# A layer's front with scaled bands and alternating pooling, and GpSimd's share of latent attention, on one Trainium2 core

## The chip, the cores and the metric

The kernel runs on one core of a Trainium2 chip. The metric is the time of one execution on the device in microseconds (us). The engines are PE (TensorE), DVE (VectorE), ACT (ScalarE), POOL (GpSimd) and SP (the queue that issues most transfers). SBUF is the on-chip memory that all of them read; PSUM, in eight banks, is where PE writes.

## The reference, cut to what matters

512 positions of width 1024, float32. A first block of two layers is followed by a second block with other mixers, which the change doesn't touch.

```python
def rms_norm(x, g):
    return x * lax.rsqrt(jnp.mean(x * x, -1, keepdims=True) + RMS_EPS) * g
...
def pool_mixer(h, w, scale):            # 4 groups of 256 channels, windows 2, 4, 8, 16
    ...
        mean = (c - lag) / jnp.minimum(n_avail, float(win))[:, None]
        outs.append(mean - hf[:, :, g])
    ...
    y = jnp.einsum('bsgc,gcd->bsgd', p, w).reshape(B, S, D)
    return y * scale
...
def mla(...):                           # 8 heads, q and k of 128 + 64 rotary dimensions
    ...
    q_rope = apply_rope(q[..., QK_NOPE_DIM:], cos[:, :, None], sin[:, :, None])
    ...
    o = causal_attention(q, k, v)
    return o.reshape(B, S, N_HEADS * V_HEAD_DIM) @ w_o

for i in range(2):
    h = rms_norm(x, norm_mix[i])
    x = x + (pool_mixer(h, ...) if i % 2 == 0 else mla(h, ...))
    h = rms_norm(x, norm_ffn[i])
    x = x + swiglu(h, w_gate[i], w_up[i], w_down[i])     # silu(h @ gate) * (h @ up) @ down
```

## The kernel before, in words

Every engine has a program of its own, written out by hand; counting semaphores order them against each other. Nothing is reordered by a scheduler: what stands first in an engine's program runs first.

**Products.** Each float32 operand is split into a high part and a low part (the residue). A product is three matmuls into one PSUM bank: high by high, low by high, high by low (`triple`, L1649, L1650, L1651). `chunk` runs 8 of these triples, 24 matmuls, for one tile of 128 output rows and all 512 positions.

**Weights** come in units of 2048 columns (1 MB). SP loads unit n into `w_raw`, slot n % 2; ACT copies it rounded to `w_hi` (`split_hi`, L614), DVE subtracts to get `w_lo` (`split_lo`, L1049). Slots are free again when the products of unit n - 2 are done. Unit 0 holds the pool weights; gate and up units of the first layer follow in turn.

**The front of layer 0.** x comes in two halves, token by row. ACT squares the four tiles of 128 tokens with their sums (L627) and takes the root; DVE takes its reciprocal (L1072) and scales each tile to `h_tok` (L1075). PE transposes x in 32 pieces (L1673) and ACT copies the eight results to `xT` (L633). The pooling of positions is itself a matmul: each 128x128 piece of `h_tok` is multiplied by a banded matrix `band` (L1685), four matmuls for each of eight channel tiles; ACT and DVE split the result (L638, L1080). The pool weights follow: `mixed`, six matmuls for each of eight tiles; DVE adds the result to `xT` (L1087), ACT and DVE split the sum times its gain to `xg_hi` and `xg_lo` (L642, L1090), ACT squares it (L645), and a matmul with ones (L1693) sums the squares over the partitions into bank 7, one for each tile. Six of those stand before the first gate chunk, two behind it. The chunks of gate and up then run; their results are divided by the root of that sum when DVE reads them, so PE need not wait for it, but bank 7 must be read once the sum is complete.

GpSimd computes the rotary angles in this time (L573 to L593) and has 6 instructions late in the second block (L600).

**The latent attention of layer 1.** Heads go in pairs; each pair has one unit of weights of 1664 columns (`heads`, four units), and seven projections: kn0, kn1, va, vb, qn0, qn1 and u, which is the rotary part of both heads' queries. A loop over 32 steps, one for each head and block of 128 queries, runs on all engines; each is some stages apart from the others. In a step PE computes scores, DVE the row maximum and `neg_max` (L1252), ACT the exponential (L764), DVE the normalising (L1259), PE the transposes of the probabilities (L1840), ACT and DVE their split (L774, L1267), PE the product with the values. `after_step` places the projections of the next pair between the steps, `rotary_head` the rotary residue. For u, DVE multiplies the PSUM result by cosine and sine, four products of 64x512 (L1219, L1220), a matmul with a fixed matrix does the turning in the scores, ACT rounds them (L736) and DVE takes the residue (L1230). DVE also does the residue of the next pair's weights in three pieces, in steps 1 to 3 of each even head. `proj_ready` counts all results DVE has read, and tells PE that a bank is free.

Behind the loop come the last heads' outputs, the unit `mla_o` + 1 to + 4 splits (ACT loads another function table before the first), and the output product `out` for eight tiles m, each over eight heads. Six heads of tiles 0 and 1 are done inside the loop.

## Time and profile before

| | us |
|---|---|
| median of 3 runs | 1404.18 (1402.97 to 1404.34) |
| the profiled execution | 1406.12 |
| its span, first to last instruction | 1404.3 |
| PE busy in it | 1328.1 |
| DVE busy | 788.8 |
| ACT busy | 536.7 |
| POOL busy | 33.0 |
| mean granted clock, 1 being 2.4 GHz | 0.983 |

"Busy" is the time in which an engine has an instruction running. An idle stretch is put down to what ended it, the "releaser". Busy times overlap, so they don't add up to the span. A row of the timeline gives start and length; "xN" means N instructions of one form in a row. Matmuls are pipelined: one of 512 columns is shown as 0.39 us but the next starts 0.23 behind it.

### The profile page before, as it was taken

The numbers are of one execution on the slowest core, as the hardware profiler recorded it, in microseconds if no ns is written. First come the engines' busy times: TensorE is split into PE (matmuls) and PEld (weight loads), VectorE is DVE, ScalarE is ACT, GpSimd is POOL, SyncE is SP. The second block draws the span as 40 slices with busy tenths as digits, with TensorE's granted clock in tenths as the row PEclk, the third lists the DMA queues.
The fourth block names the chain that finished last, engine by engine and source line by source line (L and its number), as shares of the span: only waits on it lengthen the run. The fifth ranks groups of instructions, "written<-read, shape, count | busy, mean of one in ns | idle before, by whom it ended". The sixth has DMA issues, their size and how long they took to land.

```text
span 1404.3 us, 16380 instructions
## 1 busy us (share of the span) xinstructions
PE 1328.1 (95%) x6217; PEld 1099.4 (78%) x6217; DVE 788.8 (56%) x1098; ACT 536.7 (38%) x758; POOL 33.0 (2%) x32
## 2 busy tenths in 40 slices
PE   6999999999999888899999999999999999977997
PEld 5788888888877777788888888888887787766876
DVE  5644445444458676564444444545675578876554
ACT  6522233233334444332322222343233445555334
POOL 6000000000000000000000000000000000020000
PEclk9999999999999899999999999999999999979998
DMA  5122322222331100132222322325441211102321
GB/s 207 62 90 91 118 90 90 84 91 83 101 99 55 49 31 31 60 119 92 90 90 91 118 75 83 101 83 144 130 150 61 60 48 28 61 0 99 116 71 60
DMA packets 120888, 119.43 MB, mean 85 GB/s; under 512 B 13500, under 2 KB 117896, under 8 KB 120584
## 3 DMA queue, kind: packets, MB, share of 16 engines
q1 hardware_dynamic: 120840, 118.77, 26.3%
q8 instruction: 32, 0.52, 0.1%
q14 instruction: 16, 0.13, 0.0%
HBM read 114.57 MB, written 4.19 MB: 85 GB/s over the span
## 4 chain that ended last, share of the span: by engine, by line
PE 83%; DVE 9%; ACT 4%; issue 3%; SPq 0%; DMA 0%; DVEq 0%; ACTq 0%
PE psum L1649 25%; PE psum L1650 25%; PE psum L1651 25%; DVE w_lo L1049 1%; PE psum L1998 1%; ACT w_hi L614 1%; PE psum L1984 1%; PE psum L1970 1%; DVE xg_lo L1225 1%; PE psum L2056 1%; PE psum L1693 1%; DVE du L1326 0%; PE psum L2092 0%; DVE row_top L1250 0%; PE psum L1917 0%
## 5 line engine op out<-in xcount | busy, mean ns | idle before, releaser
L1649 PE MATMUL psum<-xg_hi,w_hi 128*128 128x512 f32 x1072 | 426.1, 397 | 2.1 <-DVE xg_lo L1563 2.1
L1651 PE MATMUL psum<-xg_hi,w_lo 128*128 128x512 f32 x1072 | 417.6, 390 | 0.0
L1650 PE MATMUL psum<-xg_lo,w_hi 128*128 128x512 f32 x1072 | 417.4, 389 | 0.0
L1649 PEld LDWEIGHTS psum<-xg_hi,w_hi 128*128 128x128 f32 x1072 | 201.6, 188 | 44.6 <-DVE xg_lo L1563 3.5
L1651 PEld LDWEIGHTS psum<-xg_hi,w_lo 128*128 128x128 f32 x1072 | 201.2, 188 | 42.5
L1650 PEld LDWEIGHTS psum<-xg_lo,w_hi 128*128 128x128 f32 x1072 | 201.5, 188 | 40.6 <-issue 1.4
L1112 DVE TENSOR_TENSOR w_lo<-w_raw,w_hi 128x2048 fp32r<-128x2048 f32 x42 | 96.3, 2292 | 154.4 <-ACT w_hi L667 154.4
L1136 DVE TENSOR_TENSOR w_lo<-w_raw,w_hi 128x2048 fp32r<-128x2048 f32 x32 | 73.3, 2292 | 115.9 <-ACT w_hi L686 115.9
L1649 PE MATMUL psum<-act_hi,w_hi 128*128 128x512 f32 x352 | 137.2, 390 | 0.0
L1651 PE MATMUL psum<-act_hi,w_lo 128*128 128x512 f32 x352 | 137.0, 389 | 0.0
L1650 PE MATMUL psum<-act_lo,w_hi 128*128 128x512 f32 x352 | 136.9, 389 | 0.0
L667 ACT ACTIVATE w_hi<-w_raw 128x2048 fp32r<-128x2048 f32 x42 | 80.4, 1914 | 141.9 <-PE psum L1651 141.9
L1049 DVE TENSOR_TENSOR w_lo<-w_raw,w_hi 128x2048 fp32r<-128x2048 f32 (+4 forms) x59 | 90.8, 1540 | 29.0 <-ACT w_hi L614 28.9
L686 ACT ACTIVATE w_hi<-w_raw 128x2048 fp32r<-128x2048 f32 x32 | 61.2, 1913 | 117.6 <-PE psum L1651 117.6
L614 ACT ACTIVATE w_hi<-w_raw 128x2048 fp32r<-128x2048 f32 (+1 forms) x39 | 73.2, 1876 | 29.7 <-PE psum L1651 29.6
L1649 PEld LDWEIGHTS psum<-act_hi,w_hi 128*128 128x128 f32 x352 | 66.1, 188 | 14.2 <-DVE w_lo L1136 0.6
L1651 PEld LDWEIGHTS psum<-act_hi,w_lo 128*128 128x128 f32 x352 | 66.1, 188 | 13.8
L1650 PEld LDWEIGHTS psum<-act_lo,w_hi 128*128 128x128 f32 x352 | 66.1, 188 | 13.7
L670 ACT ACTIVATE root<-squares 128x512 f32<-128x512 f32 x44 | 27.8, 632 | 100.4 <-DVE squares L1117 100.4
L672 ACT ACTIVATE act_hi<-squares 128x512 f32 (+1 forms) x44 | 27.8, 631 | 89.0 <-DVE squares L1122 89.0
L1119 DVE TENSOR_TENSOR squares<-psum,rstd 128x512 f32<-128x512 f32 x44 | 30.4, 692 | 50.4 <-PE psum L1651 50.4
L1125 DVE TENSOR_TENSOR act_lo<-squares,act_hi 128x512 f32 (+1 forms) x44 | 30.5, 693 | 39.9 <-ACT act_hi L672 39.9
(366 smaller groups left out, 1751.6 us busy)
## 6 DMA issues: line engine op xcount, KB each, us to landing
w_raw<-in_ffn_w_gate SPq DMA_DIRECT2D x22, 1024.0 KB, 5.0
w_raw<-in_ffn_w_up SPq DMA_DIRECT2D x22, 1024.0 KB, 5.0
w_raw<-in_w_in SPq DMA_DIRECT2D x16, 1024.0 KB, 5.5
w_raw<-in_ffn_w_down SPq DMA_DIRECT2D x16, 768.0 KB, 4.8
w_raw<-in_ffn_w_down SPq DMA_DIRECT2D x16, 640.0 KB, 4.5
w_raw<-in_mla_w_o SPq DMA_DIRECT2D x4, 1024.0 KB, 5.0
w_raw<-in_w_out SPq DMA_DIRECT2D x4, 1024.0 KB, 5.1
w_raw<-in_w_ple_gate SPq DMA_DIRECT2D x4, 1024.0 KB, 5.0
```

The lines of the kernel that those rows point to most:

```text
L614: hi = act.activation(w_hi[:, n % 2, c], raw(n)[:, c], ACT.Copy)
L667: act.activation(w_hi[:, n % 2, :], raw(n), ACT.Copy).then_inc(hi_sem, 1)
L670: act.activation(gate_s, gate_z, ACT.Silu).then_inc(ga, 1)
L686: act.activation(w_hi[:, n % 2, :], raw(n), ACT.Copy).then_inc(hi_sem, 1)
L1049: lo = dve.tensor_tensor(w_lo[:, n % 2, c], raw(n)[:, c], w_hi[:, n % 2, c].bitcast(F32), ALU.subtract)
L1112: dve.tensor_tensor(w_lo[:, n % 2, :], raw(n), w_hi[:, n % 2, :].bitcast(F32), ALU.subtract).then_inc(lo_sem, 1)
L1119: dve.tensor_tensor(up_z, bank[2 + c][:, :], rstd[:, :], ALU.mult).then_inc(gd, 1)
L1125: dve.tensor_tensor(act_lo[:, f, :].rearrange("p a t -> p (a t)"), gate_z, act_hi[:, f, :].bitcast(F32).rearrange("p a t -> p (a t)"), ALU ...
L1136: dve.tensor_tensor(w_lo[:, n % 2, :], raw(n), w_hi[:, n % 2, :].bitcast(F32), ALU.subtract).then_inc(lo_sem, 1)
L1649: pe.matmul(o, wh, xh, start=start, stop=False, skip_group_check=True)
L1650: pe.matmul(o, wh, xl, start=False, stop=False, skip_group_check=True)
L1651: return pe.matmul(o, wl, xh, start=False, stop=stop, skip_group_check=True)
```

## The change

**Front.** x arrives as first half, identity, second half; four of the vectors are issued by SP and six by ACT's queue; the band comes after positions and rotary columns. Squares of tokens: tiles 0 and 2 on ACT, 1 and 3 on DVE. The reciprocal root scales the bands (`band_tok`, four instructions of 576 columns) and the pooling matmul takes x itself. x is transposed for seven tiles into seven banks; `xT` is copied by DVE (tiles 0 to 3) and ACT (4 to 7). The pool weights are split in four parts of 512 columns, placed between the splits of the pooled tiles; on PE, five pooled tiles are followed by mixed and pooled tiles by turns. The eight matmuls with ones become one: ACT writes all eight squares to `mix_squares`, DVE adds them in three instructions of 2048, 1024 and 512 columns, and PE's one matmul follows the second gate chunk. Two casts and a product of gains move behind all this on DVE.

**Attention.** For pairs 1 to 3 ACT copies u from PSUM to `rope_in`, and GpSimd computes the four products, the two rotary residues of a pair, and the weight residues: 1664 columns for pairs 1 to 3, and 2048 for the first unit of `mla_o`. Pair 0 stays with DVE.

**Behind the loop.** The splits of `mla_o` + 1 move into the loop's steps 32 (ACT) and 33 (DVE). PE does seven heads of output tile 2 (21 matmuls) before the last head's part of tiles 0 and 1.

```diff
+        mix_squares = h_tok[:, :, :].rearrange("p i (h t) -> p (i h) t", t=T)
...
+        rope_in = sq_sum2[:, :]
...
+        def proj_released(idx):
+            pr, what = PROJ_ORDER[idx]
+            if what == "u":
+                return (sem("rope_turned"), 4) if pr == 0 else (sem("rope_kept"), pr)
+            return sem("proj_ready"), proj_index(pr, what) + 1
...
+            load_vectors(sp, list(ROWS)[0:SP_VECTORS])
             sp.dma_start(pos_i[:, :], a["positions"][0:1, :].to_broadcast([P, T])).then_inc(sem("pos_loaded"), 16)
             sp.dma_start(rope_col[:, :], a["c_rope"]).then_inc(sem("pos_loaded"), 16)
+            sp.dma_start(band[:, :, :, :], a["c_band"]).then_inc(sem("band_loaded"), 16)
+            load(0)
             sp.dma_start(masks0[:, :], a["c_masks"][:, 0, :]).then_inc(sem("mask_loaded"), 16)
-            load(0)
...
+            def heads_split(n):
+                pool.wait_ge(lo_sem, n)
+                pool.wait_ge(hi_sem, n + 1)
+                c = slice(0, head_thirds(n)[-1])
+                pool.tensor_tensor(w_lo[:, n % 2, c], raw(n)[:, c], w_hi[:, n % 2, c].bitcast(F32), ALU.subtract).then_inc(lo_sem, 1)
+                pool.wait_ge(lo_sem, n + 1)
+            def rotary_products(pr):
+                pool.wait_ge(sem("rope_kept"), pr)
+                pool.wait_ge(sem("rope_lo"), 2 * pr)
+                for e in range(2):
+                    r = slice(64 * e, 64 * e + 64)
+                    for half, table in enumerate((cos_t, sin_t)):
+                        if e or half:
+                            pool.wait_ge(sem("rope_turned"), 4 * pr + 2 * e + half)
+                        pool.tensor_tensor(squares[64 * half:64 * half + 64, e, :], rope_in[r, :], table[r, :], ALU.mult)\
+                            .then_inc(sem("rope_turned"), 1)
+                pool.wait_ge(sem("rope_turned"), 4 * pr + 4)
+            def rotary_residue(h):
+                pool.wait_ge(sem("rope_hi"), h + 1)
+                pool.tensor_tensor(xg_lo[:, QR + h % 2, :], squares[:, h % 2, :], xg_hi[:, QR + h % 2, :].bitcast(F32), ALU.subtract)\
+                    .then_inc(sem("rope_lo"), 1)
+                pool.wait_ge(sem("rope_lo"), h + 1)
+            for h in range(HEADS):
+                for ii in range(NB):
+                    if rotary_head(h, ii) is not None:
+                        rotary_residue(rotary_head(h, ii))
+                    if (h // 2 + 1, "u") in after_step(h, ii):
+                        rotary_products(h // 2 + 1)
+                    if h % 2 == 0 and ii == 0:
+                        heads_split(FIRST["heads"] + 1 + h // 2)
...
+            load_vectors(act, list(ROWS)[SP_VECTORS:])
             act.preload_act_table(ACT.Sqrt)
-            for i in range(NB):
+            for i in (0, 2):
...
+            for m in range(4, KD):
+                act.wait_ge(sem("x_turned"), m + 1)
+                act.activation(xT[:, m, :], bank[m][:, :], ACT.Copy).then_inc(sem("xT_late"), 1)
...
+            def weight_split(g):
+                if g == 0:
+                    act.wait_ge(raw_sem[0], loaded(0))
+                act.activation(pool_part(w_hi, g), pool_part(w_raw, g), ACT.Copy).then_inc(*((hi_sem, 1) if g == 3 else mark(f"pool_w_hi{g}")))
...
-                act.wait_ge(sem("mix_added"), m + 1)
-                act.activation(xg_hi[:, m, :], xT[:, m, :], ACT.Copy, scale=gain("norm_ffn", m)).then_inc(sem("mix_act"), 1)
-                if m >= 2:
-                    act.wait_ge(sem("mix_summed"), m - 1)
-                act.activation(squares[:, m % 2, :], xT[:, m, :], ACT.Square).then_inc(sem("mix_act"), 1)
+                last = act.activation(mix_squares[:, m, :], xT[:, m, :], ACT.Square)
+            last.then_inc(*mark("mix_squared"))
...
+                        if pr:
+                            act.wait_ge(sem("proj_done"), idx + 1)
+                            act.activation(rope_in, proj_result(idx), ACT.Copy).then_inc(sem("rope_kept"), 1)
...
+                    if s == NB * HEADS:
+                        split_hi(FIRST["mla_o"] + 1)
...
-            dve.wait_ge(sem("ident_loaded"), 16)
-            dve.tensor_copy(ident_r[:, :], ident[:, :]).then_inc(sem("masks_ready"), 1)
-            dve.wait_ge(sem("mask_loaded"), 16)
-            dve.tensor_copy(causal[:, :], masks0[:, :]).then_inc(sem("masks_ready"), 1)
+            for i in (1, 3):
+                dve.wait_ge(sem(f"x_loaded{i // 2}"), 16)
+                dve.scalar_tensor_tensor(h_tok[:, i, :], x_tok[:, i, :], 1.0, x_tok[:, i, :], ALU.mult, ALU.mult, accum_out=tok_stat[:, 0, i:i + 1])\
+                   .then_inc(sem("tok_squares"), 1)
+            for m in range(3):
+                dve.wait_ge(sem("x_turned"), m + 1)
+                dve.tensor_copy(xT[:, m, :], bank[m][:, :]).then_inc(sem("xT_early"), 1)
+            dve.wait_ge(*at("tok_root"))
+            dve.reciprocal(tok_stat[:, 2, :], tok_stat[:, 1, :]).then_inc(*mark("tok_rstd"))
+            dve.wait_ge(*at("tok_rstd"))
+            dve.wait_ge(sem("band_loaded"), 16)
+            for i in range(NB):
+                dve.tensor_scalar(band_tok[:, i, :, :], band[:, :, int(i == 0), :], tok_stat[:, 2, i:i + 1], None, ALU.mult).then_inc(sem("band_ready"), 1)
+            dve.wait_ge(sem("x_turned"), 4)
+            dve.tensor_copy(xT[:, 3, :], bank[3][:, :]).then_inc(sem("xT_early"), 1)
...
+            mixed_add(4)
+            split_lo(1)
+            mixed_split(0)
+            for m in range(5, KD):
+                mixed_add(m)
+                mixed_split(m - 4)
+            for m in range(4, KD):
+                mixed_split(m)
...
+                if l == 0:
+                    dve.wait_ge(*at("mix_squared"))
+                    half, pair = mix_squares[:, 0:4, :], mix_squares[:, 0:2, :]
+                    dve.tensor_tensor(half, half, mix_squares[:, 4:8, :], ALU.add).then_inc(*mark("mix_halved"))
+                    dve.wait_ge(*at("mix_halved"))
+                    dve.tensor_tensor(pair, pair, mix_squares[:, 2:4, :], ALU.add).then_inc(*mark("mix_quartered"))
+                    dve.wait_ge(*at("mix_quartered"))
+                    dve.tensor_tensor(mix_squares[:, 0, :], mix_squares[:, 0, :], mix_squares[:, 1, :], ALU.add).then_inc(*mark("mix_summed"))
                 dve.wait_ge(*at(f"{tag}_root"))
...
-                        if rotary_head(h, ii) is not None:
-                            rotary(rotary_head(h, ii))
                         for t in after_step(h, ii):
                             proj(*t)
-                        if h % 2 == 0 and ii >= 1:
-                            split_lo(FIRST["heads"] + 1 + h // 2, ii - 1)
+                    if s == NB * HEADS + 1:
+                        dve.wait_ge(lo_sem, FIRST["mla_o"] + 1)
+                        split_lo(FIRST["mla_o"] + 1)
                     if s >= 6 and (s - 6) % NB == NB - 1:
                         head_out((s - 6) // NB)
                 dve.memset(sq_sum[:, :], 0.0).then_inc(*mark("attn_clear"))
                 dve.wait_ge(*at("attn_clear"))
                 for u in range(1, 5):
-                    split_lo(FIRST["mla_o"] + u)
+                    if u > 1:
...
+            for c in range(4):
+                pooled(c)
+                if c == 1:
+                    pe.wait_ge(*at("cols_ready"))
+                    turn_x(7, range(NB)).then_inc(sem("x_turned"), 1)
+            pooled(4)
+            for m in range(KD):
+                mixed(m)
+                if m < 3:
+                    pooled(m + 5)
...
+                            if first and l == j == 0 and c == 1:
+                                pe.wait_ge(*at("mix_summed"))
+                                pe.wait_ge(sem("ones_set"), 1)
+                                pe.matmul(bank[7][:, :], ones[:, :], mix_squares[:, 0, :], start=True, stop=True).then_inc(*mark("mix_stat"))
...
-                        pe.wait_ge(sem("proj_ready"), idx - 1 if idx > len(FIRST_PROJ) else 4)
+                        pe.wait_ge(*proj_released(idx - 2 if idx > len(FIRST_PROJ) else FIRST_PROJ.index("vb")))
...
+                out(2, 0, 7)
                 for m in range(KD):
-                    out(m, 6 if m < 2 else 0, HEADS)
+                    out(m, 6 if m < 2 else 7 if m == 2 else 0, HEADS)
```

The order of the instructions. VectorE before, behind the eighth pooled tile's split to the root of the squares (L1087 adds, L1090 takes residues):

```order
L1049 TENSOR_TENSOR w_lo<-w_raw,w_hi 128x2048
L1087 SCALAR_TENSOR_TENSOR xT<-psum,cols,xT 128x512 x2
L1090 SCALAR_TENSOR_TENSOR xg_lo<-xT,cols,xg_hi 128x512
...
L1090 SCALAR_TENSOR_TENSOR xg_lo<-xT,cols,xg_hi 128x512 x2
L1049 TENSOR_TENSOR w_lo<-w_raw,w_hi 128x2048
L1099 RECIPROCAL rstd<-root 128x512
```

The same place now, from the residue of weight unit 1 on (L1192 adds, L1198 takes residues):

```order
L1142 TENSOR_TENSOR w_lo<-w_raw,w_hi 128x2048
L1198 SCALAR_TENSOR_TENSOR xg_lo<-xT,cols,xg_hi 128x512
L1192 SCALAR_TENSOR_TENSOR xT<-psum,cols,xT 128x512
...
L1198 SCALAR_TENSOR_TENSOR xg_lo<-xT,cols,xg_hi 128x512 x5
L1226 CAST causal<-masks 128x128
L1228 CAST ident_r<-ident 128x128
L1230 TENSOR_TENSOR gain<-cols 128x8
L1142 TENSOR_TENSOR w_lo<-w_raw,w_hi 128x2048
L1240 TENSOR_TENSOR h_tok<-h_tok 128x2048
L1242 TENSOR_TENSOR h_tok<-h_tok 128x1024
L1244 TENSOR_TENSOR h_tok<-h_tok 128x512
L1246 RECIPROCAL rstd<-root 128x512
```

The weight residue and the three adds of the tree now stand between the last residue and the reciprocal, and unit 1's residue stands ahead of most of this, where before it stood ahead of all adds.

In the attention, VectorE before, around the rotary products of the next pair (`row_top`, `neg_max` and `probs` are the step's softmax):

```order
L1267 TENSOR_TENSOR pt_lo<-psum,pt_hi 128x3x128
L1219 TENSOR_TENSOR squares<-psum,cos_t 64x512
L1220 TENSOR_TENSOR squares<-psum,sin_t 64x512
L1219 TENSOR_TENSOR squares<-psum,cos_t 64x512
L1220 TENSOR_TENSOR squares<-psum,sin_t 64x512
L1225 TENSOR_TENSOR xg_lo<-psum,xg_hi 128x2x2x128
L1272 TENSOR_TENSOR o_lo<-psum,o_hi 128x512
L1250 TENSOR_REDUCE row_top<-psum 128x1
```

VectorE now at the same step:

```order
L1409 TENSOR_TENSOR pt_lo<-psum,pt_hi 128x3x128
L1366 TENSOR_TENSOR xg_lo<-psum,xg_hi 128x2x2x128
L1414 TENSOR_TENSOR o_lo<-psum,o_hi 128x512
L1392 TENSOR_REDUCE row_top<-psum 128x1
L1394 TENSOR_TENSOR neg_max<-row_top,rq 128x1
```

GpSimd's program in the attention for the first two units (it had nothing there before):

```order
L627 TENSOR_TENSOR w_lo<-w_raw,w_hi 128x1664
L639 TENSOR_TENSOR squares<-sq_sum,cos_t 64x512
L639 TENSOR_TENSOR squares<-sq_sum,sin_t 64x512
L639 TENSOR_TENSOR squares<-sq_sum,cos_t 64x512
L639 TENSOR_TENSOR squares<-sq_sum,sin_t 64x512
L646 TENSOR_TENSOR xg_lo<-squares,xg_hi 128x512
L627 TENSOR_TENSOR w_lo<-w_raw,w_hi 128x1664
L646 TENSOR_TENSOR xg_lo<-squares,xg_hi 128x512
```

The four products left VectorE's queue for GpSimd's, whose odd head's residue (the second L646) stands behind the next unit's weights.

## Rows read from the trace of the kernel before

**Rows 1.** The page's first part: engine, busy us (share of the span) x instructions.

```profile
PE 1328.1 (95%) x6217; PEld 1099.4 (78%) x6217; DVE 788.8 (56%) x1098; ACT 536.7 (38%) x758; POOL 33.0 (2%) x32
```

**Rows 2.** Windows, front and attention loop: window, length, busy per engine, PEclk, DMA.

```profile
0.00:60.67 60.67, 47.38 (x229) 38.16 (x230) 36.80 (x41) 37.25 (x51) 24.45 (x26) 1.00 0.40 138
449.00:557.00 108.00, 87.60 (x486) 75.82 (x487) 79.22 (x206) 53.34 (x125) 0.00 (x0) 0.94 0.12 38
```

**Rows 3.** Waits, 0 to 16 us: engine line <- releaser: total us, times, longest.

```profile
PE psum L1666 <- DMA vec_rows<-in_conv_b: 10.1, 1, 10.1
```

**Rows 4.** Waits, 446 to 580 us, the attention loop and what follows.

```profile
PE psum L1840 <- DVE pt_lo L1267: 10.3, 10, 2.2
...
PE psum L1649 <- DVE xg_lo L1225: 4.8, 6, 1.1
...
PE psum L1649 <- issue: 3.2, 2, 1.8
```

**Rows 5.** Timeline of the front: start us, us, engine line op out<-in xcount [idle before <-releaser].

```profile
13.38 2.79 DVE L1075 TENSOR_SCALAR h_tok<-x_tok,tok_stat 128x1024 f32<-128x1024 f32 x3
...
15.66 1.09 ACT L633 ACTIVATE xT<-psum 128x512 f32<-128x512 f32 x2
...
39.64 1.02 PE L1693 MATMUL psum<-squares,ones 128*128 128x512 f32 x2
...
40.10 0.80 PE L1649 MATMUL psum<-pooled_hi,w_hi 128*128 128x512 f32 x1
...
43.22 0.80 PE L1649 MATMUL psum<-xg_hi,w_hi 128*128 128x512 f32 x1
...
44.63 1.90 ACT L614 ACTIVATE w_hi<-w_raw 128x2048 fp32r<-128x2048 f32 x1
...
46.56 2.29 DVE L1049 TENSOR_TENSOR w_lo<-w_raw,w_hi 128x2048 fp32r<-128x2048 f32 x1 [1.57 <-ACT w_hi L614]
...
56.26 0.39 PE L1649 MATMUL psum<-xg_hi,w_hi 128*128 128x512 f32 x1
...
61.70 0.39 PE L1649 MATMUL psum<-xg_hi,w_hi 128*128 128x512 f32 x1
```

**Rows 6.** Groups of VectorE, 446 to 580 us: shapes, xcount | busy, mean ns | idle.

```profile
L1049 DVE TENSOR_TENSOR w_lo<-w_raw,w_hi 128x512 fp32r<-128x512 f32 (+3 forms) x13 | 11.4, 879 | 2.9 <-ACT w_hi L614 2.9
...
L1252 DVE TENSOR_TENSOR neg_max<-row_top,rq 128x1 f32<-128x1 f32 x32 | 5.1, 159 | 1.1
...
L1219 DVE TENSOR_TENSOR squares<-psum,cos_t 64x512 f32<-64x512 f32 x6 | 4.1, 686 | 1.1 <-issue 1.0
```

**Rows 7.** Timeline, GpSimd's instructions and VectorE's beside them.

```profile
34.40 1.29 POOL L591 TENSOR_TENSOR angle<-angle 128x512 f32<-128x512 f32 x1
...
34.84 1.39 DVE L1090 SCALAR_TENSOR_TENSOR xg_lo<-xT,cols,xg_hi 128x512 fp32r<-128x512 f32 x1
...
1247.43 8.96 POOL L600 TENSOR_TENSOR pn_lo<-du,pn_hi 64x512 fp32r<-64x512 f32 x6 [1210.72 <-ACT pn_hi L867]
...
1250.11 1.11 DVE L1532 TENSOR_SCALAR du<-du,row_inv 128x1024 f32<-128x1024 f32 x1
```

**Rows 8.** Timeline, weights and first projection of pair 1, u to scores of pair 3.

```profile
450.46 0.82 DVE L1049 TENSOR_TENSOR w_lo<-w_raw,w_hi 128x640 fp32r<-128x640 f32 x1 [0.79 <-ACT w_hi L614]
...
454.45 0.50 PE L1649 MATMUL psum<-ckv_hi,w_hi 128*128 128x512 f32 x1 [1.23 <-DVE w_lo L1049]
...
521.17 0.39 PE L1651 MATMUL psum<-cq_hi,w_lo 128*128 128x512 f32 x1
...
524.97 0.47 PE L1649 MATMUL psum<-cq_hi,w_hi 128*128 128x512 f32 x1 [1.79 <-issue]
...
529.47 0.50 PE L1649 MATMUL psum<-xg_hi 128*128 128x512 f32 x1 [1.01 <-DVE xg_lo L1225]
```

**Rows 9.** Timeline of TensorE behind the loop.

```profile
573.58 0.50 PE L1649 MATMUL psum<-o_hi,w_hi 128*128 128x512 f32 x1 [0.67 <-DVE o_lo L1272]
...
578.48 0.50 PE L1649 MATMUL psum<-o_hi,w_hi 128*128 128x512 f32 x1 [2.53 <-DVE w_lo L1049]
```

More of the change, by code:

```diff
@@ new lines, in mixed_split @@
+            def mixed_split(m):
+                act.wait_ge(sem("mix_added"), m + 1)
+                act.activation(xg_hi[:, m, :], xT[:, m, :], ACT.Copy, scale=gain("norm_ffn", m)).then_inc(sem("mix_hi"), 1)
+            act.wait_ge(*at("cols_ready"))
+            weight_split(0)
+            pooled_split(0)
+            pooled_split(1)
+            weight_split(1)
+            pooled_split(2)
+            pooled_split(3)
+            weight_split(2)
+            pooled_split(4)
+            weight_split(3)
@@ L1068, in _, with weight_split, pooled_split @@
             dve.wait_ge(*at("cols_ready"))
+            def weight_split(g):
+                dve.wait_ge(*((hi_sem, 1) if g == 3 else at(f"pool_w_hi{g}")))
+                dve.tensor_tensor(pool_part(w_lo, g), pool_part(w_raw, g), pool_part(w_hi, g).bitcast(F32), ALU.subtract)\
+                   .then_inc(*((lo_sem, 1) if g == 3 else mark(f"pool_w_lo{g}")))
+            def pooled_split(c):
+                dve.wait_ge(sem("pooled_hi"), c + 1)
+                dve.scalar_tensor_tensor(pooled_lo[:, c, :], bank[POOLED_BANKS[c]][:, :], gain("norm_mix", c), pooled_hi[:, c, :].bitcast(F32),
+                                         ALU.mult, ALU.subtract).then_inc(sem("pooled_lo"), 1)
@@ new lines, in mixed_add, with mixed_split @@
+            def mixed_add(m):
+                if m == 0:
+                    dve.wait_ge(sem("xT_early"), 4)
+                if m == 4:
+                    dve.wait_ge(sem("xT_late"), 4)
+                dve.wait_ge(sem("mixed_done"), m + 1)
+                dve.scalar_tensor_tensor(xT[:, m, :], bank[4 + m % 3][:, :], gain("pool_scale", m), xT[:, m, :], ALU.mult, ALU.add)\
+                   .then_inc(sem("mix_added"), 1)
+            def mixed_split(m):
+                dve.wait_ge(sem("mix_hi"), m + 1)
+                dve.scalar_tensor_tensor(xg_lo[:, m, :], xT[:, m, :], gain("norm_ffn", m), xg_hi[:, m, :].bitcast(F32),
+                                         ALU.mult, ALU.subtract).then_inc(sem("mix_lo"), 1)
@@ L1661, in chunk, with turn_x @@
                 return mm
+            def turn_x(m, blocks):
+                for i in blocks:
+                    mm = pe.transpose(bank[m][:, i * P:(i + 1) * P], x_tok[:, i, m * P:(m + 1) * P], ident[:, :])
+                return mm
             pe.wait_ge(sem("ident_loaded"), 16)
+            pe.wait_ge(sem("x_loaded0"), 16)
+            for m in range(7):
+                turn_x(m, (0, 1))
+            pe.wait_ge(sem("x_loaded1"), 16)
+            for m in range(7):
+                turn_x(m, (2, 3)).then_inc(sem("x_turned"), 1)
@@ L1684, in _ @@
                     n = min(BAND, T - i * P)
-                    mm = pe.matmul(bank[4 + c % 4][:, i * P:i * P + n], h_tok[:, i, c * P:(c + 1) * P], band[:, c // 2, int(i == 0), 0:n],
+                    mm = pe.matmul(bank[POOLED_BANKS[c]][:, i * P:i * P + n], x_tok[:, i, c * P:(c + 1) * P], band_tok[:, i, c // 2, 0:n],
                                    start=i == 0, stop=i == NB - 1, skip_group_check=True)
                 mm.then_inc(sem("pooled_done"), 1)
-            def mix_squares(m):
-                if m == 0:
-                    pe.wait_ge(sem("ones_set"), 1)
-                pe.wait_ge(sem("mix_act"), 2 * m + 2)
-                pe.matmul(bank[7][:, :], ones[:, :], squares[:, m % 2, :], start=m == 0, stop=m == KD - 1, skip_group_check=True).then_inc(sem("mix_summed"), 1)
@@ L1696, in _, with mixed @@
[L1696 to L1699 removed]
+            def mixed(m):
                 g, c = divmod(m, 2)
[L1701 to L1702 removed]
+                wh, wl = hi_tiles(0, 8)
+                pe.wait_ge(*((lo_sem, 1) if g == 3 else at(f"pool_w_lo{g}")))
+                pe.wait_ge(*((sem("xT_late"), m + 1) if m < 3 else (sem("mix_added"), m - 2)))
```

168 lines of the change are left out of this document (75 added, 93 removed).

## The prediction

> **What bounds the kernel now.** I read the page first: TensorE is busy 95% of the span [rows 1]. It is the bound nearly everywhere, so only places where TensorE stands idle, or does work that can be left out, can give time. I then asked for windows over the two stretches that the change touches. In the first 60.67 us TensorE is busy 47.38 us: 13.3 us are open. In the 108 us of the attention loop it is busy 87.60: 20.4 us are open, with VectorE at 79.22, ScalarE at 53.34 and GpSimd at nothing [rows 2]. The waits say what is behind it. At the start TensorE stands 10.1 us for the vectors [rows 3]; in the loop and just behind it 10.3 us for residues of transposed probabilities, 4.8 for residues of projections, 3.2 for "issue", which stands where a projection waits for the bank that VectorE's rotary products read [rows 4]. So the loop is held by VectorE's queue in small pieces, not by its busy share.
>
> The profiled execution took 1406.12 us (span 1404.3). The sum below is made against that span; the median of the runs, 1404.18, lies 1.9 lower, so a span change goes onto the median unchanged. What a measurement here can tell from no change is 0.2%, 2.8 us.
>
> **Part 1, the front.** Before: h_tok (0.93 us a tile, from 13.38) feeds pooling. Mixed products begin only behind the eighth tile, and of the eight ones matmuls six stand among and behind them, two behind the first gate chunk. A ones matmul costs 0.86: 0.46 to the next start (39.64 to 40.10), and the first product behind it 0.4 more than the 0.23 of the others. The first gate chunk starts at 43.22. A chunk is 24 matmuls, 5.44 us (56.26 to 61.70), and the fourth (the second of the up unit) starts at 61.70 [rows 5].
>
> After, walked with these durations (0.7 to 0.75 for a residue or add of 512 columns, 0.66 from start to start):
> - The transposes no longer stand behind the vectors, and hide beside the statistics. Squares end about 9.6 (two engines instead of one), root 9.9, three copies on VectorE, reciprocal 11.8. Four bands of 576 columns, taken at 0.69 from h_tok's 0.93 for 1024, end at 14.6. Pooling starts at 14.9 instead of 15.8.
> - Pooled tile 4, pool weight parts (0.69 each) and residues (0.70) lead to mixed(0) at 20.7. TensorE then owes three pooled tiles and five mixed products, six matmuls or 1.36 us each, and waits for VectorE between: mixed(4) ends near 29.5, its add at 30.1.
> - VectorE next does the residue of weight unit 1, 2.29 us, then six alternating adds and residues at 0.66: 36.5. The first gate chunk can run from 34.7 instead of 43.22.
> - **The new tail of the front**: ScalarE's last xg_hi at 37.2, eight squares at 0.53 (back to back, from 1.09 for two copies) to 41.5, w_hi of unit 2 1.90 to 43.4; VectorE's w_lo 2.29 to 45.7; then the three adds of the tree, 2048, 1024 and 512 wide, 2.29 + 1.2 + 0.69 and their gaps, to 50.0. TensorE has both gate chunks behind it at 46.5 and waits 3.5 us for this sum. The one ones matmul (0.86) is over at 50.9 and the third chunk (5.44) at 56.3; the fourth starts there, against 61.70. **Gain 5.4 us.** Seven ones matmuls less are in it. All else of the front (DMA order, casts moved behind, gain product) lies beside this: the cast of ident is needed in attention first.
>
> Bounds: 6.7 if the tree runs without gaps and squares a little faster; 3.4 if the band, now behind more issues on SP, or the weights come 2 us late.
>
> **Part 2, GpSimd in the attention.** VectorE loses 11.4 us of weight residues (2.29 of them only moved within the tail), twice 4.1 of rotary products (one of the two lines stands in the rows) and six rotary residues of the same 0.69: about 21 us of its 79 [rows 6]. GpSimd gets 12 products of 64x512 at 1.4 (between 1.29, a product of 128x512 alone, and 1.49, a sixth of the 8.96 that six took), six residues at 1.29, three weight residues of 1664 columns at 4.2 (1.29 x 1664/512) and one of 2048 at 5.2: 42.3 us in all [rows 7], none of which was there. What then ends TensorE's waits:
> - *Rotary chain, once in each of three pairs.* Before, the last matmul of u starts at 521.17 and the scores that need the residue start at 529.47 [rows 8]: 7.9 us behind its end, in which TensorE waits 1.79 and 1.01. After: ScalarE copy 0.6, four products 5.6, residue 1.3, hops 0.3: 7.8 us. A wait of much the same length remains. It is at another place, and the odd head's residue, behind GpSimd's next residue of weights, adds 0.7 each time. Waits for rotary and bank: 8.0 before, 12.4 after.
> - *First pair's weights.* VectorE began the residue at 450.46 and did it in three pieces with softmax between; TensorE waited 1.23 for it, until 454.45 [rows 8]. GpSimd in one piece of 4.2 ends at 454.7: +0.3.
> - *Probabilities.* VectorE, at 54% instead of 73%, answers sooner. Of 11 us of waits for pt_lo I take 3.9 as gone, those with a moved instruction ahead in its queue.
> - Sum so far +0.6 to +0.8.
> - *VectorE beside GpSimd.* A VectorE residue from two SBUF inputs, begun at 34.84, took 1.39 instead of the usual 0.74 while GpSimd's product ran from 34.40 to 35.69 [rows 7]: as if it had stood until that was over. In the loop neg_max is such an operation, 32 times on the path from scores to exponential [rows 6]. GpSimd busy 42.3 of 108 us meets 13 of them; the rest of the instruction that they meet is 1.3 us on average (a random point falls oftener into the long weight residues): 17 us held. Each step lasts 3.4 us and VectorE works 1.8 in it, so most is absorbed. Ends: 0 and 17; I take 2.4, a seventh, since the one wait of this kind in the trace cost TensorE nothing that can be seen.
>
> **Loop: +3.0 us**, with ends -6 (all waits for pt_lo and projections go) and +14.
>
> The Trainium skill, "SBUF — State Buffer", section "SBUF: two separate sides", says that VectorE and GpSimd share a port under an exclusive lock, held for the whole instruction when VectorE needs both. The rows above agree. By it, VectorE's normalising of probabilities would be held too, and the sum for the loop would be +10.
>
> **Part 3, behind the loop.** TensorE waited 0.67 at 573.58 and 2.53 at 578.48 for w_lo of mla_o's second unit [rows 9]. The change makes it inside the loop and puts 21 matmuls ahead of the last heads' outputs. Both waits (3.2) go; the third unit's residue, behind the same ScalarE table load, is late next, by 1.0 to 1.5 as TensorE comes sooner. **Gain 2.2** (1.7 to 3.2).
>
> **Sum**: -5.4 + 3.0 - 2.2 = -4.6. Span 1399.7, median 1399.6. The granted clock was 0.94 in the loop [rows 2]; a spell at 1.2 GHz more or less moves this by 1 to 2 us.
>
> **Rivals.**
> 1. *The loop gains as well* (0.15). VectorE's load falls by a quarter and the waits for pt_lo and xg_lo go, 15 us with the bank waits; rotary waits on GpSimd return 8 and holding 3: -4 instead of +3. For it: each of these waits is behind VectorE's queue. Against: the rotary chain is no shorter. -5.4 - 4 - 2.2: 1392.6.
> 2. *The front gives little* (0.21), that is, the change doesn't do what it says there. The sum of squares has moved from eight hidden pieces to one chain of 12.8 us that TensorE waits for; with GpSimd's angle chain beside it, a late band, or half clock behind a 3.5 us pause, it ends 3 us later: -2.2 + 3.0 - 2.2, 1402.8.
> 3. *GpSimd holds VectorE* (0.14), the other side. In the loop neg_max and the normalising wait out whole GpSimd instructions, up to 5.2 us. The price is +10 to +12 in place of +3.0; it decides from +7.6 on, where front and tail are used up; at +11 the sum is +3.4: 1407.6. For it: the row of 1.39. Against: VectorE's scaling with one SBUF input, at 1250.11 amid six GpSimd products, took 1.11 [rows 7], less than one of those.
>
> **How the numbers follow.** Forecast 0.50, covering 1397 to 1402.5. Predicted 1399.6. The range takes in rival 1 down to 1392 and rival 3's nearer half to 1407. Faster by over 2.8 us (under 1401.4): most of the forecast (0.44) and rival 1 (0.15), 0.59. Within 2.8: the forecast's upper edge, nearly all of rival 2 and the mild end of rival 3, 0.28. Slower: the rest, 0.13.
>
> **What the profile of the changed kernel would show.** Right: first gate chunk near 34.7, a TensorE wait of about 3.5 us for the ones matmul, the fourth chunk near 56.3; GpSimd near 75 us busy; waits on GpSimd's rotary residue of 2 to 3.5 us three times; pt_lo waits of 6 to 9 us; no wait of 2.5 behind the loop. Wrong: GpSimd's products far over 1.5 us, neg_max over 1 us many times, a wait over 6 us before the ones matmul, or loop waits well off 23.

## The result, and the profile after

The changed kernel takes 1412.35 us (median of 5 runs, 1411.12 to 1413.80), the kernel before 1402.97 (5 runs, 1400.30 to 1404.34): ratio 1.0069, 95% interval 1.0058 to 1.0080. It is **slower by 9.4 us**; 4.6 less was forecast. The profiled executions differ by less, spans 1410.5 and 1404.3, and the traces below are compared by those: the one of the kernel before took 1406.12 us, 3.2 above its median, so a few us of every comparison with its trace may be that execution's own.

The page's first part, after (against [rows 1]): GpSimd has gained 35 us of work, and VectorE is no less busy.

```profile
PE 1332.8 (94%) x6203; PEld 1105.6 (78%) x6203; DVE 791.8 (56%) x1082; ACT 533.0 (38%) x756; POOL 68.4 (5%) x54
```

**The front, timeline after** (against [rows 5]):

```profile
13.01 2.85 DVE L1167 TENSOR_SCALAR band_tok<-band,tok_stat 128x576 f32<-128x576 f32 x4 [1.30 <-DMA band<-in_c_band]
13.68 4.91 PE L1831 MATMUL psum<-band_tok,x_tok 128*128 128x144 f32 x16 [2.29 <-DVE band_tok L1167]
...
36.55 0.42 PE L1791 MATMUL psum<-xg_hi,w_hi 128*128 128x512 f32 x1
...
40.32 4.26 ACT L734 ACTIVATE h_tok<-xT 128x512 f32<-128x512 f32 x8
...
48.63 2.28 DVE L1240 TENSOR_TENSOR h_tok<-h_tok 128x2048 f32<-128x2048 f32 x1
...
52.96 1.13 PE L1885 MATMUL psum<-h_tok,ones 128*128 128x512 f32 x2 [3.42 <-DVE h_tok L1244]
...
59.40 0.39 PE L1791 MATMUL psum<-xg_hi,w_hi 128*128 128x512 f32 x1
```

The steps stand in the forecast order, and TensorE waits 3.42 us for the sum (forecast 3.5), but all of it is later: VectorE waits 1.30 us behind the reciprocal for the band, and the granted clock from 13 to 21 us is 0.57. The first gate chunk starts at 36.55 (forecast 34.7), the fourth chunk at 59.40 (forecast 56.3, before 61.70). The front gives 2.3 us of the 5.4.

**The loop**, from the first row maximum to the last, the same 492 matmul records in each run. The windows of the kernel before and of the change, columns as in [rows 2]:

```profile
447.16:555.51 108.35, 88.24 (x492) 76.50 (x490) 79.33 (x204) 53.69 (x125) 0.00 (x0) 0.94 0.12 38
```

```profile
444.84:562.54 117.70, 93.82 (x492) 81.75 (x490) 76.69 (x174) 55.20 (x128) 39.15 (x22) 0.87 0.11 35
```

It is 9.35 us longer. TensorE's open time (the time in which no matmul runs) grows by 3.8 (20.1 to 23.9), its busy time for the same matmuls by 5.6, at a granted clock of 0.87 instead of 0.94: about 31 us of this loop ran at 1.2 GHz, and about 13 before. The same window of e1 below, which has the new front and tail but none of GpSimd's work, is shorter than both:

```profile
445.73:547.63 101.90, 82.53 (x492) 71.71 (x490) 79.18 (x204) 53.51 (x125) 0.00 (x0) 1.00 0.14 40
```

Against it the change opens 4.5 us more and its matmuls take 11.3 longer. VectorE has 30 instructions less and hardly less busy time. The groups of VectorE from 445 to 563 us say where it went (mean ns stands behind the busy time):

```profile
L1401 DVE TENSOR_SCALAR probs<-probs,row_inv 128x512 f32<-128x512 f32 (+3 forms) x30 | 21.7, 722 | 1.1
...
L1394 DVE TENSOR_TENSOR neg_max<-row_top,rq 128x1 f32<-128x1 f32 x32 | 12.6, 394 | 1.1
```

neg_max took 5.1 us in all before [rows 6] and takes 12.6. The normalising before, in the group of 446 to 580 us:

```profile
L1259 DVE TENSOR_SCALAR probs<-probs,row_inv 128x512 f32<-128x512 f32 (+3 forms) x32 | 12.4, 387 | 1.1
```

It takes 722 ns each now, 335 more. That is 7.5 and 10 us, against 21 taken away. Nine of the 32 neg_max took over 0.25 us, the longest 1.73. Timeline of one place, VectorE and GpSimd:

```profile
474.92 3.95 POOL L627 TENSOR_TENSOR w_lo<-w_raw,w_hi 128x1664 fp32r<-128x1664 f32 x1 [9.55 <-ACT w_hi L678]
475.16 0.55 DVE L1409 TENSOR_TENSOR pt_lo<-psum,pt_hi 128x384 fp32r<-128x384 f32 x1
...
477.37 0.41 DVE L1392 TENSOR_REDUCE row_top<-psum 128x1 f32<-128x256 f32 x1
477.82 1.07 DVE L1394 TENSOR_TENSOR neg_max<-row_top,rq 128x1 f32<-128x1 f32 x1
478.81 0.15 DVE L1399 RECIPROCAL row_inv<-row_sum 128x1 f32<-128x1 f32 x1
...
478.95 1.26 POOL L646 TENSOR_TENSOR xg_lo<-squares,xg_hi 128x512 fp32r<-128x512 f32 x1
479.00 1.44 DVE L1401 TENSOR_SCALAR probs<-probs,row_inv 128x384 f32<-128x384 f32 x1
```

neg_max, one column wide and 0.16 us long when alone, ends 0.02 us behind GpSimd's instruction; the normalising (0.4 to 0.5 alone) ends 0.23 behind GpSimd's next one. The residue and the maximum that read PSUM run through at their usual 0.55 and 0.41. Waits of TensorE, 440 to 590 us, after (against [rows 4]; pt_lo is the residue of the transposed probabilities, xg_lo that of a projection):

```profile
PE psum L1986 <- DVE pt_lo L1409: 15.9, 13, 2.8
...
PE psum L1791 <- issue: 5.8, 3, 2.8
...
PE psum L1986 <- DVE probs L1401: 1.7, 1, 1.7
```

The waits for pt_lo grew from 10.3 to 15.9; "issue" is now the wait for GpSimd's rotary residue. Those for xg_lo are gone. The last row is new: the first weight residue held a normalising for 3.20 us, and TensorE waited 1.7 for it.

### The profile page after: what moved, and what is told of

It is laid out like the page before. It is cut to its first block, busy times and chain, and to the rows that moved or that the text cites. A ratio compares the mean times of both kernels' runs of the same rounds, so it can differ in the third digit from the quotient of the medians.

```text
span 1410.5 us, 16349 instructions
## 1 busy us (share of the span) xinstructions
PE 1332.8 (94%) x6203; PEld 1105.6 (78%) x6203; DVE 791.8 (56%) x1082; ACT 533.0 (38%) x756; POOL 68.4 (5%) x54
## 4 chain that ended last, share of the span: by engine, by line
PE 82%; DVE 10%; ACT 4%; issue 3%; DMA 1%; SPq 0%; POOL 0%; DVEq 0%; ACTq 0%
PE psum L1791 25%; PE psum L1792 25%; PE psum L1793 25%; DVE w_lo L1142 1%; PE psum L2145 1%; ACT w_hi L678 1%; PE psum L2131 1%; PE psum L2117 1%; DVE probs L1401 1%; PE psum L1831 1%; PE psum L1986 1%; DMA band<-in_c_band 1%; PE psum L2203 1%; DVE du L1468 0%; PE psum L2239 0%
## 5 line engine op out<-in xcount | busy, mean ns | idle before, releaser
L1142 DVE TENSOR_TENSOR w_lo<-w_raw,w_hi 128x2048 fp32r<-128x2048 f32 (+3 forms) x46 | 79.2, 1722 | 26.1 <-ACT w_hi L678 26.1
L1791 PEld LDWEIGHTS psum<-act_hi,w_hi 128*128 128x128 f32 x352 | 66.1, 188 | 14.4 <-DVE w_lo L1283 0.6
L1792 PEld LDWEIGHTS psum<-act_lo,w_hi 128*128 128x128 f32 x352 | 66.1, 188 | 13.6
```

Of the source, the lines that this page charges most:

```text
L1142: lo = dve.tensor_tensor(w_lo[:, n % 2, c], raw(n)[:, c], w_hi[:, n % 2, c].bitcast(F32), ALU.subtract)
L1791: pe.matmul(o, wh, xh, start=start, stop=False, skip_group_check=True)
L1792: pe.matmul(o, wh, xl, start=False, stop=False, skip_group_check=True)
```

## The experiments

Each group of experiments was timed beside its own runs of the kernel before, whose medians were 1402.28 (e1 to e4), 1402.69 (e5 to e8), 1403.43 (e9 to e12) and 1404.14 (e13 to e16). The table gives ratios to those, and for the loop, between the same two instructions as above, its length, TensorE's busy time in it and the granted clock. Medians come from all runs of a kernel, the last three columns from one traced execution each.

| run | front | rotary | weight residues | median us | ratio (95%) | loop | PE busy | clock |
|---|---|---|---|---|---|---|---|---|
| before | old | VectorE | VectorE | 1402.97 | | 108.4 | 88.2 | 0.94 |
| change | new | GpSimd | GpSimd | 1412.35 | 1.0069 (1.0058-1.0080) | 117.7 | 93.8 | 0.87 |
| e2, old tail | new | VectorE | VectorE | 1397.65 | 0.9969 (0.9954-0.9984) | 104.4 | 85.4 | 0.97 |
| e1 | new | VectorE | VectorE | 1397.93 | 0.9967 (0.9954-0.9979) | 101.9 | 82.5 | 1.00 |
| e3 | new | GpSimd | VectorE | 1397.46 | 0.9965 (0.9951-0.9978) | 103.6 | 85.5 | 0.96 |
| e4 | new | VectorE | GpSimd, whole | 1408.67 | 1.0041 (1.0027-1.0054) | 114.3 | 89.5 | 0.93 |
| e5 | new | VectorE | GpSimd, 128 | 1395.85 | 0.9946 (0.9933-0.9958) | 102.1 | 83.3 | 0.98 |
| e11 | new | VectorE | as e5, first VectorE | 1393.78 | 0.9931 (0.9915-0.9946) | 99.3 | 82.1 | 1.00 |
| e16 | new | VectorE | as e11, 256 | 1393.81 | 0.9930 (0.9917-0.9944) | 99.6 | 82.0 | 1.00 |
| e9 | new | GpSimd | GpSimd, 128 | 1414.56 | 1.0076 (1.0062-1.0091) | 120.3 | 93.6 | 0.87 |
| e10 | new | GpSimd | as e9, first VectorE | 1409.61 | 1.0051 (1.0036-1.0066) | 114.0 | 89.1 | 0.93 |
| e13 | new | GpSimd, ahead | GpSimd, 128 | 1399.57 | 0.9977 (0.9968-0.9986) | 106.6 | 86.3 | 0.95 |
| e15 | new | GpSimd, ahead | as e13, first VectorE | 1398.18 | 0.9957 (0.9943-0.9971) | 103.5 | 84.9 | 0.97 |
| e14 | new | GpSimd, ahead | GpSimd, whole | 1418.28 | 1.0103 (1.0088-1.0118) | 124.2 | 95.1 | 0.86 |
| e12, neg_max on ScalarE | new | GpSimd | GpSimd, whole | 1403.09 | 0.9997 (0.9986-1.0008) | 106.9 | 85.6 | 0.95 |

**Parts alone.** e1 undoes GpSimd's share:

```diff
-                    if rotary_head(h, ii) is not None:
-                        rotary_residue(rotary_head(h, ii))
-                    if (h // 2 + 1, "u") in after_step(h, ii):
-                        rotary_products(h // 2 + 1)
-                    if h % 2 == 0 and ii == 0:
-                        heads_split(FIRST["heads"] + 1 + h // 2)
...
+                        if rotary_head(h, ii) is not None:
+                            rotary(rotary_head(h, ii))
...
+                        if h % 2 == 0 and ii >= 1:
+                            split_lo(FIRST["heads"] + 1 + h // 2, ii - 1)
```

> The change without GpSimd's share of the attention: VectorE does the rotary products, their residues and the weight residues in three pieces, as before; the front and the part behind the loop stay changed. Theory H (GpSimd's instructions hold VectorE's neg_max and normalising): the loop is as before, the front gives 2.3 and the tail 2.1 as in the trace of the change, so 4 to 5 us below before, and no neg_max over 0.2 us. Theory R (the rotary chain itself became longer): the same here. Theory C (the clock fell in the loop for another reason, such as the earlier start): the loop stays some 5 us longer, and the time is at or above before.

e2 also restores the part behind the loop; e3 and e4 take back only one half of GpSimd's share.

> The front alone. From the two traces: 2.3 us gained at the second turn of gate and up, so 2 to 3 us below before. If the front had given what was forecast it would be 5.4. The spell at half clock at 13.6 us should be there again if the front's own order makes it.

> As e1, but GpSimd does the rotary products and residues (18 instructions of 1.28 us); weight residues on VectorE. H: it meets neg_max and normalising some 8 times with 0.6 us each and costs 3 to 6 us over e1; the longest neg_max is below 1.4 us. R: all of the 11 us that the loop lost is here.

> As e1, but GpSimd does the weight residues (three of 3.9 us, one of 4.6); rotary on VectorE. H: few but long holds, a normalising of 3 us and neg_max of over 1.5 us; costs 3 to 6 us over e1. R: VectorE is relieved and nothing else changes, so it is at or below e1.

Without GpSimd the change gains 4.4 us, as H said; C falls. Its loop is not "as before", though: 6.5 us shorter in the traces with the same instructions, at a granted clock of 1.00. The front alone (e2) gives 4.6, more than the 2 to 3 expected, and the same as e1, so the part behind the loop gives nothing that these runs can tell. Rotary on GpSimd costs nothing, against both theories, although it held neg_max six times for over 0.25 us, up to 1.21. The weight residues, four instructions of 16.2 us in all, cost 10.7 us, well over H's 3 to 6, and R falls. In e4 each of them held one VectorE instruction: the first a normalising (3.20 us), the others a rotary residue that takes 0.69 alone (3.13, 3.14, 3.81). None of them was a neg_max, against what H said: all 32 took 5.1 us, as before. What stood behind the held instruction in VectorE's queue came late all the same; TensorE's waits for pt_lo in the loop are 13.6 us, in e1 7.8:

```profile
473.70 3.94 POOL L627 TENSOR_TENSOR w_lo<-w_raw,w_hi 128x1664 fp32r<-128x1664 f32 x1 [20.76 <-ACT w_hi L674]
...
475.06 3.13 DVE L1368 TENSOR_TENSOR xg_lo<-squares,xg_hi 128x512 fp32r<-128x512 f32 x1 [0.56 <-ACT xg_hi L819]
```

**Length of GpSimd's instruction.** e5 does the same residues in pieces:

```diff
-                pool.tensor_tensor(w_lo[:, n % 2, c], raw(n)[:, c], w_hi[:, n % 2, c].bitcast(F32), ALU.subtract).then_inc(lo_sem, 1)
+                for c0 in range(0, c.stop, 128):
+                    c1 = slice(c0, min(c0 + 128, c.stop))
+                    part = pool.tensor_tensor(w_lo[:, n % 2, c1], raw(n)[:, c1], w_hi[:, n % 2, c1].bitcast(F32), ALU.subtract)
+                part.then_inc(lo_sem, 1)
```

> As e4 (weight residues on GpSimd, rotary on VectorE), but each residue in pieces of 128 columns, one instruction each. Theory H (VectorE is held until the running GpSimd instruction ends, and gets its turn between two): the longest normalising falls from 3.2 to under 0.9 us and the time to within 3 us of e1. Theory B (both engines share what the memory gives, whatever the length): the time stays at e4's, some 10 us above e1. If GpSimd wins every turn, normalising stays at 3 us and the time too.

12.8 us less than e4, and 2 less than e1. The columns, the data and the place are the same; GpSimd even works longer (25.4 us instead of 16.2 in the loop). So what costs is the length of a hold, not shared bandwidth. Timeline of e5:

```profile
472.28 6.24 POOL L629 TENSOR_TENSOR w_lo<-w_raw,w_hi 128x128 fp32r<-128x128 f32 x13 [19.18 <-ACT w_hi L677]
...
473.63 0.69 DVE L1371 TENSOR_TENSOR xg_lo<-squares,xg_hi 128x512 fp32r<-128x512 f32 x1 [0.56 <-ACT xg_hi L822]
...
475.29 0.21 DVE L1393 TENSOR_TENSOR neg_max<-row_top,rq 128x1 f32<-128x1 f32 x1
...
475.61 0.51 DVE L1400 TENSOR_SCALAR probs<-probs,row_inv 128x384 f32<-128x384 f32 x1
```

VectorE gets its turn between two pieces. One new wait stood in e5, 3.1 us for the first unit's residue:

```profile
PE psum L1792 <- POOL w_lo L629: 3.1, 1, 3.1
```

e11 gives that one unit back to VectorE, e16 takes pieces of 256.

> As e5 (rotary on VectorE, weight residues in pieces on GpSimd), but VectorE does the first weight residue: the wait of 3.1 us goes and VectorE's queue takes 2.2 us more. 0 to 2 us below e5's 1395.9, so about 1394.5.

> As e11, the best so far, with pieces of 256 columns instead of 128: a hold lasts up to 0.7 us instead of 0.4, and GpSimd is done some 1.3 us earlier. Within 1.5 us of e11's 1393.8.

Both as expected (e11 2.1 us below e5, e16 level with it), and the best of all: 0.69% and 0.70% under the kernel before.

**The full change, mended.** e9 is the change with the pieces alone, e10 with the first unit on VectorE too.

> The changed kernel with one edit: GpSimd's weight residues in pieces of 128 columns. Rotary stays on GpSimd, in whole instructions of 1.28 us. Theory H: the long holds are what made it slow, so it falls from 1412 to between 1396 and 1401. If the two parts of GpSimd's work harm each other in another way (a rotary residue queued behind the weight residue), it stays above 1405: in pieces the weight residue takes 5.7 to 7.3 us instead of 3.7 to 4.6, so that queue is longer.

> As e9, but VectorE does the first of the four weight residues, in its three pieces. In e5 TensorE waited 3.1 us for that one alone. 1 to 3 us below e9.

e9 gained nothing, and its waits show why:

```profile
PE psum L1794 <- issue: 13.9, 6, 3.6
PE psum L1989 <- DVE pt_lo L1412: 8.8, 11, 2.1
PE psum L1794 <- POOL w_lo L629: 3.0, 1, 3.0
```

The pieces did their part: the waits for pt_lo fell from 15.9 us to 8.8. But there are six waits for rotary residues instead of the three of 5.8 us in the change, and one for the first unit's residue. e10 is 5.0 us below e9 (1 to 3 expected). Timeline of GpSimd and of TensorE at one of the new ones:

```profile
476.31 5.76 POOL L629 TENSOR_TENSOR w_lo<-w_raw,w_hi 128x128 fp32r<-128x128 f32 x13 [8.57 <-ACT w_hi L681]
482.14 1.26 POOL L649 TENSOR_TENSOR xg_lo<-squares,xg_hi 128x512 fp32r<-128x512 f32 x1
```

```profile
483.51 0.47 PE L1794 MATMUL psum<-xg_hi 128*128 128x512 f32 x1 [2.31 <-issue]
```

The odd head's residue is queued behind the weight residue, and that now takes 5.76 us instead of 3.95. e13 and e14 let it go first, with pieces and without:

```diff
-                    if h % 2 == 0 and ii == 0:
+                    if h % 2 == 0 and ii == 1:
                         heads_split(FIRST["heads"] + 1 + h // 2)
```

> As e9 (full change, weight residues in pieces of 128), but GpSimd does the odd head's rotary residue ahead of the weight residue. Theory Q (the queue on GpSimd is what e9 and e10 pay): the three waits for the odd heads' residues go and the time falls by 8 us or more, to 1400 to 1406. If the holds by the rotary instructions pay for it, it stays above 1410.

> The changed kernel with that one move, weight residues whole. If both theories hold, the queue's part goes and the holds' part stays: 1405 to 1409. Theory H alone: no change from 1412. Theory Q alone: the same as e13.

> As e13, with the first weight residue on VectorE: 2 to 5 us below e13 (e9 to e10 gave 5).

e13 is 15 us below e9: Q holds there, and the two mended together make the full change faster than before (0.9977). The waits for the odd heads' residues are gone:

```profile
PE psum L1794 <- issue: 5.7, 3, 2.8
```

e15 is 1.4 below e13, less than the 2 to 5 expected. With the residues in pieces rotary on GpSimd is no longer free, as it was in e3: e13 and e15 stand about 4 us above e5 and e11, which have it on VectorE (ratios 0.9977 and 0.9957 against 0.9946 and 0.9931). No run says why.

e14 is 6 above the change, against every theory's number: for whole residues the queue cost nothing, and the move brought the long instruction over neg_max itself:

```profile
478.12 3.71 POOL L627 TENSOR_TENSOR w_lo<-w_raw,w_hi 128x1664 fp32r<-128x1664 f32 x1
```

```profile
478.18 3.67 DVE L1394 TENSOR_TENSOR neg_max<-row_top,rq 128x1 f32<-128x1 f32 x1
```

A product of one column takes 3.67 us; the next transposes on TensorE wait 3.46 for what follows from it. The change differs from e14 only in the place of the weight residue in GpSimd's program, and so in what it holds.

**Which VectorE instruction.** e12 gives neg_max to ScalarE:

```diff
-                    dve.wait_ge(sem("att_top"), s + 1)
-                    dve.tensor_tensor(neg_max[:, c], row_top[:, c], rq[:, 1, 2 * i:2 * i + 1], ALU.mult).then_inc(sem("att_max"), 1)
...
+                    act.wait_ge(sem("att_top"), s + 1)
+                    act.activation(neg_max[:, c], row_top[:, c], ACT.Copy, scale=rq[:, 1, 2 * i:2 * i + 1]).then_inc(sem("att_max"), 1)
```

> The changed kernel with one edit: ScalarE computes neg_max, so VectorE has no operation from two SBUF inputs in a step; the normalising stays where it is. If neg_max's holds (some 7 us of 18 in the trace of the change) carry the cost, it falls by 4 us or more; if the holds of the normalising do, it stays within 2 us of 1412.

9.3 us less. The normalising is still held, if less (18.6 us for 30; 21.7 in the change, 11.8 before), so getting neg_max out of VectorE's queue is worth most of the loss. That does not make neg_max's own holds the dear ones: e4 has none and loses 10.7, e3 has six of up to 1.21 us and loses nothing. What is dear comes with GpSimd's instructions of 3.7 to 4.6 us: in e4 and e14 holds of 3.1 us and more, in the change one such hold and then three of 1.1 to 1.7 on neg_max, each followed at once by 1.4 for the normalising under the rotary residue queued behind. The edit also takes VectorE's own work on neg_max away, about 5 us; the two are not told apart here.

**The front's waits.**

```diff
             pe.wait_ge(sem("x_loaded1"), 16)
             for m in range(7):
-                turn_x(m, (2, 3)).then_inc(sem("x_turned"), 1)
+                turn_x(m, range(NB)).then_inc(sem("x_turned"), 1)
...
-                            if first and l == j == 0 and c == 1:
+                            if first and l == 0 and j == 1 and c == 0:
```

> As e1, but all transposes of the seven tiles wait for the second half of x, so that TensorE starts about 2.4 us later and idles less before pooling. If the early start followed by the wait for the bands brings the half clock near 16 us (3.4 to 6.8 us), it is gone and the gate chunks start up to 2 us sooner; if the spell comes from the pooling matmuls themselves, it stays and the time is that of e1 within 1 us.

> As e1, but the ones matmul stands behind the third chunk (first of the up unit) instead of the second. TensorE then doesn't wait 3.4 us for the sum, and the half clock near 53 us goes with the wait. Up to 3.4 + 1.7 us gained if the later root and reciprocal don't hold the next turn; if they do, 0 to 2 us gained.

> Both edits of e6 and e7. If they are independent the gains add.

e6 (the first edit, which drops the loop over the first half too) took 1398.42 us: the granted clock from 10 to 22 us is 1.00, and the time is e1's all the same, which neither branch of the expectation had. The first mixed product starts 1.4 us earlier than in e1 (20.52 against 21.91), the first gate chunk only 0.3 (35.56 against 35.84). The timeline of e6 shows where the rest went:

```profile
30.95 1.30 POOL L617 TENSOR_TENSOR angle<-angle 128x512 f32<-128x512 f32 x1
31.33 3.07 DVE L1134 TENSOR_TENSOR w_lo<-w_raw,w_hi 128x2048 fp32r<-128x2048 f32 x1
32.34 2.54 POOL L619 TENSOR_SCALAR angle<-angle 128x512 f32<-128x512 f32 x1
```

VectorE's residue, 2.28 us in e1, now meets one of GpSimd's angle products and takes 3.07; GpSimd's next instruction, 0.61 in e1, starts inside that residue and takes 2.54. It is the loop's hold again, here in both directions.

e7 (the second) took 1399.45 and e8 (both) 1400.63, no gain where some was expected (ratios 0.9974 and 0.9984, against e1's 0.9967): the wait of 3.4 us for the sum turned into one of 3.9 for the next turn's bank, since VectorE can't read the first turn's results before that sum:

```profile
PE psum L1790 <- DVE squares L1256: 3.9, 1, 3.9
```

## Why the prediction was wrong, point by point

- **Front, -5.4: right in kind, too large.** Measured 2.3 in the trace. The steps that failed are those up to VectorE's residue of weight unit 1, forecast to begin at 30.1 and begun at 33.41. "Four bands ... end at 14.6" took them to start at 11.8 (measured 13.0, the band landed late), pooling was taken at full clock (granted 0.57 of it), and ScalarE's 1.90 us for that unit (from 28.17) was not counted ahead of a pooled tile's split, for which VectorE waited 1.47. From there on VectorE's and ScalarE's walk keeps its distance of about 3 us; the later terms (eight squares 4.3 us, tree to the sum, wait 3.5) were measured at 4.26, 4.27 and 3.42. e6 shows that these delays don't add: full clock alone gained nothing. In medians the front alone (e2) gives 4.6, but e2's trace doesn't show that in the front: its fourth chunk starts at 60.14, 1.6 earlier than before, and its loop is 3.9 us shorter with the same instructions there, at a clock of 0.97 instead of 0.94. How much of that is the traced execution of the kernel before, 3.2 us above its median, stays open.
- **Loop, +3.0: the failed step** is "Ends: 0 and 17; I take 2.4, a seventh". The hold itself was named. Its 17 us came out by luck: they were forecast for neg_max alone, which was held for 7.5; the other 10 fell on the normalising, which the sum left out. That "most is absorbed" was wrong for the long ones. All four weight residues brought TensorE a wait behind them, of 1.7, 1.9, 1.9 and 2.8 us (the longest for pt_lo in the loop before was 1.2). e1 against the change, both with the new front and tail, is 14.4 us, e4's weight residues alone 10.7, and in pieces they cost nothing (e5).
- **The clock was counted at 1 to 2 us, and here the sum failed too.** By open time alone +3.0 was near: it grew 3.8 us against the kernel before and 4.5 against e1. The rest of the loss is the same 492 matmuls at the lower clock, 5.6 us against the kernel before and 11.3 against e1. From e11 to e14 open time grows 17.2 to 29.1 us and busy time 82.1 to 95.1. That the waits bring the clock down is argued from this, not shown.
- **The other terms of the loop were off, and made up for each other.** Waits for rotary and bank were to go from 8.0 to 12.4 and went to 5.8, with those for xg_lo gone: the chain through GpSimd was no dearer, as e3 puts its whole cost at nothing. The first pair's weights (+0.3) gave +0.5: a wait of 1.2 went and the 1.7 behind the held normalising came. The waits for pt_lo were to fall by 3.9, since VectorE would have less to do, and rose by 5.6. Together -2.2, +0.5 and +5.6 make 3.9, about the 3.8 by which open time grew.
- **Behind the loop, -2.2: right in the traces, not in the medians.** From the last row maximum to the last add of the output product it is 55.9 us before and in e2, 53.7 after and 53.8 in e1. But e1 and e2 have the same median: from that add to the end e1's trace takes 794.3 us and e2's 791.3. Nothing was changed there; that the clock gives it back is argued from 0.95 against 0.96 over the last 354 us, not shown.
- **Rivals.** Rival 3, GpSimd holds VectorE, is what happened: its price of 10 to 12 stands against 9.35 in the trace and 14.4 in medians, and it had a chance of 0.14. The row of 1.39 us, which spoke for it, was the whole mechanism. The row against it, a scaling of 1.11 us from 1250.11, was read as no hold because it is shorter than a GpSimd product. The product under it had begun earlier:

```profile
1249.41 1.26 POOL L600 TENSOR_TENSOR pn_lo<-du,pn_hi 64x512 fp32r<-64x512 f32 x1
```

It ends at 1250.67 and the scaling 0.55 behind it; the residue of 1.39 had ended 0.54 behind its product. So this row was a hold as well, and spoke for the rival. Rival 2's late front happened as well, in part.

- The Trainium skill, "SBUF — State Buffer", "SBUF: two separate sides", says that of the two engines the one that starts second is blocked until the other's instruction is over. The runs agree: the neg_max begun 0.06 us into GpSimd's 3.71 ends 0.02 behind it. The +10 that went by the rule was nearer to the trace's 9.35 than the +3.0 that went by the trace's one harmless case, though it was not worked out, and over half of the 9.35 is the clock.

## What to carry to other kernels

Before work goes to GpSimd beside a VectorE chain, list VectorE's instructions with two SBUF inputs and its SBUF to SBUF scalings, and ask for each on the critical chain what one whole GpSimd instruction ahead of it costs. If that hurts, cut GpSimd's work into short pieces (0.47 us each in e11; 0.77 in e16 did as well, and whole rotary instructions of 1.28 cost nothing in e3), and look at what is then queued behind the pieces; in the full change both were needed. A freed share of VectorE says nothing: VectorE lost 21 us of work in the loop and its busy time there fell by 2.6.

## What the hardware showed that I had not expected

- A hold takes no account of size: one column waits for the end of GpSimd's instruction just as 512 do (3.67 and 3.13 us; alone 0.16 and 0.69).
- Cutting a GpSimd residue of 1664 columns into 13 costs GpSimd 1.9 us (3.73 to 5.66), which is cheap beside what it saves.
- TensorE's granted clock differs between stretches that are nearly equally busy: 0.86 to 1.00 in a loop of the same matmuls, with 17 to 29 us of open time in 99 to 124. No single wait there was longer than 4.4 us. Over the table, runs that wait more also have slower matmuls, about one us for each us of open time. That is no rule for a pair: e3 has less open time than e1 (18.1 against 19.4 us) and more busy time (85.5 against 82.5), and the kernel before, e2 and e1, whose loops have the same instructions, stand at 88.2, 85.4 and 82.5. The clock was never changed by itself. In e1, e11 and e16 the loop's granted clock was 1.00, that is 2.4 GHz.
